# Solved 32x32 blocks brought back by products with the identity, and a filter transform cut in four parts

## What is computed

```
def second_block(x, ...):
    for i in range(2):
        x = x + 0.5 * swiglu(rmsnorm(x))
        # projections of rmsnorm(x)
        o_dn = deltanet_group(q, k, v, z, beta, alpha)   # 4 heads, both directions
        o_hy = hyena_group(...)                           # 2 long convolutions
        x = x + concat([o_dn, o_hy]) @ w_out
        x = x + 0.5 * swiglu(rmsnorm(x))
```

```
a_mat = where(strict, (k * beta) @ k.T * decay, 0) + eye(c)
u, w  = triangular_solve(a_mat, [v * beta, k * beta * exp(g)])
```

## Time and profile before

| | us |
|---|---|
| median of three runs | 3780.5 |
| the profiled execution: its time | 3779.45 |
| the profiled execution: its span in the trace | 3777.7 |
| TensorE busy | 3666.6 |
| VectorE busy | 2021.8 |
| ScalarE busy | 1081.1 |
| GpSimd busy | 70.8 |

### The profile page before, as it was taken

How to read it: one execution, slowest core, us unless ns; L and a number is a source line. 1 busy time by engine, 2 the same in 40 slices (tenths; PEclk the granted TensorE clock), 3 DMA queues, 4 the chain that set the end, 5 groups by cost and what they waited for, 6 DMA issues and landing times.

```text
span 3777.7 us, 43120 instructions
## 1 busy us (share of the span) xinstructions
PE 3666.6 (97%) x17650; PEld 2965.0 (78%) x17650; DVE 2021.8 (54%) x2565; ACT 1081.1 (29%) x1212; POOL 70.8 (2%) x80
## 2 busy tenths in 40 slices
PE   9999999999999999999998899999999998999998
PEld 8878888867788887888876678888888875768887
DVE  6564434454654445434775865434443767675432
ACT  3342222252422222222343132222222243322221
POOL 0000000000000000000010000000000102000000
PEclk9999999999999999999999999999999999999999
DMA  4212222111222222223312122222222413122221
GB/s 150 102 67 93 96 92 101 70 44 45 90 96 100 89 101 89 100 95 113 122 32 95 79 96 93 100 92 98 100 89 100 144 56 101 68 78 93 97 95 73
DMA packets 67764, 342.99 MB, mean 91 GB/s; under 512 B 23748, under 2 KB 23748, under 8 KB 32048
## 3 DMA queue, kind: packets, MB, share of 16 engines
q1 hardware_dynamic: 59696, 302.98, 22.7%
q0 software_dynamic: 5760, 37.86, 2.7%
q10 hardware_dynamic: 2176, 0.26, 0.0%
HBM read 324.30 MB, written 16.78 MB: 90 GB/s over the span
## 4 chain that ended last, share of the span: by engine, by line
PE 87%; DVE 10%; ACT 2%; issue 1%; DMA 1%; ACTq 0%; SPq 0%; DVEq 0%
PE ACC L1020 26%; PE ACC L1022 26%; PE ACC L1021 26%; DVE BX L3031 1%; DVE BT L3029 1%; DVE PT L3224 1%; PE ACC L1446 1%; DVE PT L3222 1%; PE MIX L1760 0%; DVE WL L2385 0%; PE MIX L1497 0%; PE ACC L1692 0%; PE MIX L1333 0%; PE MIX L1517 0%; PE MIX L1205 0%
## 5 line engine op out<-in xcount | busy, mean ns | idle before, releaser
L1020 PE MATMUL ACC<-HH,WH 128*128 128x512 f32 (+1 forms) x3322 | 1303.3, 392 | 19.4 <-issue 6.5
L1022 PE MATMUL ACC<-HH,WL 128*128 128x512 f32 (+1 forms) x3322 | 1288.0, 388 | 0.0
L1021 PE MATMUL ACC<-HL,WH 128*128 128x512 f32 (+1 forms) x3322 | 1287.9, 388 | 0.0
L2385 DVE TENSOR_TENSOR WL<-RAW,WH 128x2048 fp32r<-128x2048 f32 (+3 forms) x291 | 645.6, 2218 | 461.1 <-ACT WH L1854 460.6
L1020 PEld LDWEIGHTS ACC<-HH,WH 128*128 128x128 f32 x3322 | 624.8, 188 | 165.7 <-issue 18.2
L1021 PEld LDWEIGHTS ACC<-HL,WH 128*128 128x128 f32 x3322 | 625.2, 188 | 130.2 <-issue 5.0
L1022 PEld LDWEIGHTS ACC<-HH,WL 128*128 128x128 f32 x3322 | 625.1, 188 | 128.7
L1854 ACT ACTIVATE WH<-RAW 128x2048 fp32r<-128x2048 f32 (+3 forms) x291 | 536.1, 1843 | 578.8 <-PE ACC L1022 578.6
L2505 DVE TENSOR_TENSOR SG<-ACC,RS 128x512 f32<-128x512 f32 x132 | 91.3, 691 | 627.1 <-PE ACC L1022 626.8
L1020 PE MATMUL ACC<-HIDH,WH 128*128 128x512 f32 x1056 | 410.8, 389 | 0.0
L1021 PE MATMUL ACC<-HIDL,WH 128*128 128x512 f32 x1056 | 410.8, 389 | 0.0
(11 more groups left out here) (521 smaller groups left out, 2834.2 us busy)
## 6 DMA issues: line engine op xcount, KB each, us to landing
RAW<-wall SPq DMA_DIRECT2D x260, 1024.0 KB, 4.7
RAW<-wall SPq DMA_DIRECT2D x24, 768.0 KB, 4.1
KR<-spectra POOLq DMA_DIRECT2D x4, 2048.0 KB, 9.2
x_kept<-X POOLq DMA_DIRECT2D x2, 2048.0 KB, 6.6
FWK<-mats POOLq DMA_DIRECT2D x4, 1024.0 KB, 5.4
spectra<-SQ POOLq DMA_DIRECT2D x8, 512.0 KB, 3.0
spectra<-T POOLq DMA_DIRECT2D x8, 512.0 KB, 3.5
X<-x_kept POOLq DMA_DIRECT2D x2, 2048.0 KB, 14.5
```

What stands on the lines that cost most here:

```text
L1020: pe.matmul(out_ap, wh, hh, start=first, stop=False)
L1021: pe.matmul(out_ap, wh, hl, start=False, stop=False)
L1022: return pe.matmul(out_ap, wl, hh, start=False, stop=last)
L2385: v.tensor_tensor(WL[n % 2][:, 0:cols], RAW[n % 2][:, 0:cols], WH[n % 2][:, 0:cols], ALU.subtract).then_inc(w_lo, 1)
```

## The change

The trip through DRAM is gone: `blocks_out`, `blocks_back` and their semaphores, the issues of SyncE and ScalarE. In its place:

- `turn_solved` on TensorE: for each of 32 columns x, both directions d and four blocks b, a product of a 32x32 piece of `BX` with 16 columns of the identity, written to banks 2 (direction 0) and 3 (direction 1) of ACC. That is 256 products, each 32 contraction rows, 32 output rows, 16 columns. It waits for `blocks_solved` and for ScalarE to have emptied ACC.
- `solved_forward` on VectorE: four copies of 32 partitions x 512 elements from bank 2 into the diagonal blocks of `XI[:, 0]`; four of the same size on ScalarE from bank 3 into `XI[:, 1]`. `left` now waits for both (`xi_fwd`, `xi_bwd`) and no longer for the transposes; `right` waits for the transposes (`dn_xt`). For direction 1 `XI` is now filled and `XIT` is the transpose, so GpSimd clears `XI[:, 1]`, after the first two parts of the last transform (`kf_half`) and after the issue of two more stores.
- the last `filter_spectrum(1, 1)` is cut in four parts of two products each: two ahead of `turn_solved`, one behind it, one between `left` and `right` of level 0. Both `keep_clock` are gone. On ScalarE `keep_spectrum(1, 1)` goes behind the two `copy_left`.
- `YS` of the first half of the heads gets a place of its own, since the old one lies over the tables that the last parts of the transform still read.

```
-                    sp.wait_ge(blocks_solved, L + 1)
-                    sp.dma_start(blocks_out, BX[:]).then_inc(solved_sent, 16)
-                    sp.wait_ge(solved_sent, 16 * (L + 1))
-                    sp.wait_ge(dn_zero, 3 * L + 3)
-                    blocks_back(sp, 0, 0)
-                    blocks_back(sp, 1, 0)
-                    blocks_back(sp, 1, 1)
...
-                        if n == 4:
-                            pool.wait_ge(kf_sp, 4 * l + 2)
-                            pool.memset(XIT[:, 1], 0.0).then_inc(dn_zero, 1)
+                        if n == 6:
+                            pool.wait_ge(kf_half, l + 1)
+                            pool.memset(XI[:, 1], 0.0).then_inc(dn_zero, 1)
...
+        def diagonal(d, b):
+            rows = slice(64 * d + 32 * (b // 2), 64 * d + 32 * (b // 2) + 32)
+            return rows, slice(64 * d + 16 * b, 64 * d + 16 * b + 16), slice(32 * b, 32 * b + 32)
+        def solved_in(d, b):
+            return ACC[32 * b:32 * b + 32, 2 + d, :].rearrange("p (x m) -> p m x", m=16)
...
+                def turn_solved():
+                    pe.wait_ge(blocks_solved, L + 1)
+                    pe.wait_ge(kf_ev, 8 * L + 6)
+                    for x in range(32):
+                        for d in range(2):
+                            for b in range(4):
+                                held, wanted, to = diagonal(d, b)
+                                col = BX[held, :, x] if d == 0 else BX[held, x, :]
+                                mm = pe.matmul(ACC[to, 2 + d, 16 * x:16 * x + 16], col, ident[held, wanted], start=True, stop=True)
+                    mm.then_inc(solved_turned, 1)
...
-                for o in range(2):
-                    for fc in range(2):
-                        filter_spectrum(o, fc)
-                pe.wait_ge(kf_ev, 8 * L + 6)
-                keep_clock(ACC[:, 0, :], 12)
+                filter_spectrum(0, 0)
+                filter_spectrum(0, 1)
+                filter_spectrum(1, 0)
+                pe.wait_ge(kf_ev, 8 * L + 4)
+                spectrum_part(1, 1, 0, 0)
+                spectrum_part(1, 1, 0, 1).then_inc(kf_half, 1)
+                turn_solved()
+                spectrum_part(1, 1, 1, 0)
                 left(0, 0, 0)
                 left(0, 1, 0)
-                pe.wait_ge(kf_ev, 8 * L + 8)
-                keep_clock(MIX[:, 0, :], 10)
+                spectrum_part(1, 1, 1, 1).then_inc(kf_sp, 1)
                 right(0, 0, 0)
...
                 grown_keys(0, 0)
                 act.wait_ge(dn_zero, 3 * L + 3)
-                act.wait_ge(solved_sent, 16 * (L + 1))
-                blocks_back(act, 0, 1)
-                keep_spectrum(1, 1)
+                act.wait_ge(solved_turned, L + 1)
+                for b in range(4):
+                    rows = slice(32 * b, 32 * b + 32)
+                    k = act.activation(XI[rows, 1, :, rows], solved_in(1, b), ACT.Copy)
+                k.then_inc(xi_bwd, 1)
                 copy_left(0, 0, 0)
                 copy_left(0, 1, 0)
+                keep_spectrum(1, 1)
                 grown_keys(0, 1)
...
+                def solved_forward():
+                    v.wait_ge(solved_turned, L + 1)
+                    for b in range(4):
+                        rows = slice(32 * b, 32 * b + 32)
+                        k = v.tensor_copy(XI[rows, 0, :, rows], solved_in(0, b))
+                    k.then_inc(xi_fwd, 1)
+                    v.wait_ge(xi_fwd, L + 1)
...
                 def turn_blocks(p):
-                    v.wait_ge(solved_landed[p], 128 * (L + 1))
-                    v.wait_ge(kf_sp, 4 * L + 4)
+                    v.wait_ge(xi_bwd, L + 1)
```

More of the change, by code:

```diff
@@ L678, in build @@
         blocks_solved = sem("blocks_solved")
-        solved_sent = sem("solved_sent")
-        solved_landed = [sem(f"solved_landed{i}") for i in range(2)]
+        solved_turned = sem("solved_turned")
+        xi_fwd = sem("xi_fwd")
+        xi_bwd = sem("xi_bwd")
+        kf_half = sem("kf_half")
         dn_xt = sem("dn_xt")
@@ L858, in build @@
         KG = put("KG", [P, 2, 2, TC, P])
-        YS = put("YS", [P, 2, 2, TC, P])
+        YS = [place("YS0", [P, 2, 2, TC, P], at=raw_at + 4 * 4096), put("YS1", [P, 2, 2, TC, P])]
         assert put.at[0] <= mem_at
         blocks_in = nc.dram_tensor("blocks_in", (P, 32, 32), F32).ap()
-        blocks_out = nc.dram_tensor("blocks_out", (P, 32, 32), F32).ap()
         put = arena(hy_low)
@@ L1401, in left @@
                     if lev == 0:
-                        pe.wait_ge(dn_xt, 4 * L + h + 1)
+                        pe.wait_ge(xi_fwd, L + 1)
+                        pe.wait_ge(xi_bwd, L + 1)
                         pe.wait_ge(dn_at, 4 * L + h + 1)
@@ L1419, in right @@
                     if lev == 0:
+                        pe.wait_ge(dn_xt, 4 * L + h + 1)
                         for c in range(TC):
@@ L1422, in right @@
                                 for near, far in joined(d, lev):
-                                    mm = pe.matmul(ACC[far, 2 * a + d, columns(c, near)], XIT[far, d, TC * h + c, far], YS[far, a, d, c, near],
+                                    mm = pe.matmul(ACC[far, 2 * a + d, columns(c, near)], XIT[far, d, TC * h + c, far], YS[p][far, a, d, c, near],
                                                    start=True, stop=True)
@@ L1434, in right_turned @@
                             for near, far in joined(d, lev):
-                                mm = pe.matmul(ACC[near, 2 * a + d, columns(c, far)], YS[far, a, d, c, near], XIT[far, d, TC * h + c, far],
+                                mm = pe.matmul(ACC[near, 2 * a + d, columns(c, far)], YS[p][far, a, d, c, near], XIT[far, d, TC * h + c, far],
                                                start=True, stop=True)
@@ L1518, in filters_made, with spectrum_part @@
                     mm.then_inc(kf_f, 1)
+                def spectrum_part(o, fc, cs, p):
+                    bank = (ACC, MIX)[fc]
+                    for kc in range(2):
+                        q = 2 * p + kc
+                        src = FS0[:, cs, q, :] if o == 0 else FS1[:, q, :] if cs == 0 else (FS1A, FS1B)[q // 2][:, q % 2, :]
+                        mm = pe.matmul(bank[:, 2 * cs + p, :], FWK[:, cs, p, kc, fc * P:fc * P + P], src,
+                                       start=(kc == 0), stop=(kc == 1))
+                    return mm
                 def filter_spectrum(o, fc):
-                    bank = (ACC, MIX)[fc]
                     if o == 0:
@@ L1528, in filter_spectrum @@
                         for p in range(2):
[L1529 to L1533, removed]
-                    mm.then_inc(kf_sp, 1)
+                            mm = spectrum_part(o, fc, cs, p)
+                    mm.then_inc(kf_sp, 1)
+                def turn_solved():
[8 more added lines that the diff above has]
+                    mm.then_inc(solved_turned, 1)
                 sums_of_g(0)
@@ L1579, in pe_delta @@
                 pe.wait_ge(dn_qe, 8 * L + 8)
+                pe.wait_ge(kf_ev, 8 * L + 8)
                 values(0, 0)
@@ L2161, in copy_left @@
                     act.wait_ge(dn_y, 8 * L + 4 * p + 2 * lev + a + 1)
-                    act.activation(YS[:, a].rearrange("p d c n -> p d (c n)"), ACC[:, 2 * a:2 * a + 2, :], ACT.Copy).then_inc(dn_yc, 1)
+                    act.activation(YS[p][:, a].rearrange("p d c n -> p d (c n)"), ACC[:, 2 * a:2 * a + 2, :], ACT.Copy).then_inc(dn_yc, 1)
                 def copy_keys(p, a):
@@ L3041, in turn_blocks @@
                         v.transpose(XIT[:, 0, m].rearrange("p c n -> p (c n)"), XI[:, 0, m].rearrange("p c n -> p (c n)"))
-                        v.transpose(XI[:, 1, m].rearrange("p c n -> p (c n)"), XIT[:, 1, m].rearrange("p c n -> p (c n)")).then_inc(dn_xt, 1)
+                        v.transpose(XIT[:, 1, m].rearrange("p c n -> p (c n)"), XI[:, 1, m].rearrange("p c n -> p (c n)")).then_inc(dn_xt, 1)
                 def corner(tile, a, h, d, rows, cols):
@@ L3107, in dve_delta @@
                 solve_blocks()
+                solved_forward()
                 turn_blocks(0)
```

## The result

The changed kernel is slower: 3785.67 us median of 20 runs against 3777.93 us of 20 runs of the kernel before. The ratio is 1.0019, 95% interval 1.0013 to 1.0026, so 7.7 us with an interval of about 5 to 10. The forecast was 3778.3 us beside a median of 3780.5 us, so 2.2 us faster; over 20 runs that median is 2.6 us lower, and only the differences can be compared: 2.2 us faster was forecast, 7.7 us slower came. The time lies inside the stated range. At 0.19% it stands on the border of the forecast's classes "within 0.2%" (0.61) and "slower" (0.17), with an interval that is clear of no change.

A forecast was written before the change was run, and what follows sets the result against it. TensorE, busy 97% of the span, was taken as the bound. 3779.45 - 3.0 (way from "solved" to right) + 0.8 (clock charge) = 3777.25 us, or 3778.3 us beside the runs' median; range 3769.5 to 3790 us.

The forecast's parts named there:

- within 0.2%: Outcome class: a time within about 0.2% (7.6 us), which a measurement can't tell from no change; chance 0.61.
- slower: Outcome class: slower than the kernel before by more than about 0.2% (7.6 us); chance 0.17.
- Step 2: turn_solved's burst of 512 pairs: 5.6 us at full clock (11 ns a pair), 7.2 us with most at half.
- a burst over 9 us: Sign of being wrong: turn_solved's 512 pairs take over 9 us, where 5 to 8 us would show the forecast right.
- a slow fetch of the 1024 added instructions: Rival, joined with both transform parts at half clock: no gain, 3780 to 3784 us; joint chance 0.20.
- Steps 1, 3 and 4: Half the transform ends just ahead of "solved"; PSUM copies take 2.65 us on VectorE; TensorE's list, not data, releases right.
- step 5: Clock falls to half 1.2 us into the burst, returns about the third part's end; layers gain 3.0 us to right.
- Step 6: Behind right the 8.84 us to keys_solved stay; 0.4 us a layer charged for the full clock's uncertain return.
- The products don't overlap: Rival: turn_solved pairs on the same array rows run singly, 31 ns each, 15.6 us burst; 3793 to 3799 us; chance 0.16.
- The clock holds: Rival: small tiles without a pause keep TensorE at full clock; 3769 to 3773 us; chance 0.24.

The follow-up runs named there:

- loop: Changed kernel with turn_solved as a loop of 8 turns over the same 4 columns plus one more column, 528 pairs: 3777.18 us, ratio 0.9998.
- half: Changed kernel without the products of 16 of the 32 columns of turn_solved, 256 pairs a layer in place of 512: 3770.21 us, ratio 0.9985.
- rows_change: Changed kernel with the same products reordered so that neighbours never use the same 32 rows of the array: 3783.92 us, ratio 1.0017.
- idle_burst: vector_turn with the 256 products put back on TensorE ahead of the dummies and left, read by nobody: 3793.25 us, ratio 1.0041.
- idle_loop: idle_burst with the products as a loop of 8 turns over four columns and one column more, 528 pairs: 3780.33 us, ratio 1.0010.
- vector_turn: Changed kernel with blocks turned by two VectorE transposes instead of TensorE products, TensorE and ScalarE orders changed too: 3765.99 us, ratio 0.9964.
- cut_alone: Kernel before, DRAM trip kept, with only the last transform cut in parts, second keep_clock gone, keep_spectrum and YS moved: 3776.22 us, ratio 0.9994.

## Why the prediction was wrong, by its steps

- **Step 2, the burst, is the one that failed.** I took the pace of bursts of 32 and 64 pairs (11 to 15 ns) for 512 pairs and said 7.2 us. The pace was right, 11.7 ns, even at half clock, where I had 15. The three pauses were missing: 7.4 and 6.1 us. Layer 0 took 13.2 us, 6.0 more than forecast, layer 1 4.7 more, 10.7 us in all. The prediction has a gain of 3.0 us for the way to `right` and the traces a loss of 7.9: 10.7 of the 10.9 us between them are this step. Of the prediction's signs of being wrong it is the one that came, "a burst over 9 us". Where nearly no code is new (loop), 528 pairs took 7.6 us, close to my 7.2 for 512: the array was priced well, and what I put at nothing was the arrival of the code. That the pauses are the fetch of code is shown by one run that keeps the number of products and takes the code away (loop), one that halves both (half), one that changes only the order of the products (rows_change), and by the pair idle_burst and idle_loop, where nothing waits for the results. The trace's packets say the same: each of the 20 pauses inside the bursts of the changed kernel, half, rows_change and idle_burst ends 1.2 to 1.6 us after a packet of the fetch queue has landed.
- I had named "a slow fetch of the 1024 added instructions" beside a rival worth 3780 to 3784 us, without a price of its own. The rows for one were there: the page's 98 packets with 1.61 MB make 16 KB a packet, and 1024 instructions are four of these; in this kernel 256 instructions had never been executed in less than several us, so no row showed how fast such packets can follow. The right bound would have been open above, and the rival a separate one. In its cause this rival was the right one; against the median it started from it gave at most 3.5 us lost, and 7.7 came.
- Steps 1, 3 and 4 held, and step 5 in the main. Half of the transform ended at "solved". VectorE's copies took 2.79 us (2.65), ScalarE's 2.38 (2.4). The clock fell 2.9 us into the burst of layer 0, where I had 1.2, and in a pause of TensorE that I hadn't foreseen; in loop, without pauses, it fell 4.4 us in. It came back at the end of the third part in layer 0, and 1.2 us later, at the end of `left`, in layer 1. From the end of the burst to `right`: 6.1 us in layer 0 and 6.7 in layer 1 (6.25). ScalarE's slack ahead of the level-1 `copy_left` was 1.01 us (1 us).
- Step 6: from `right` to `keys_solved` 8.84 us, as before. `keys_solved` took 4.77 us for 5.82 in layer 0 and 5.27 for 5.79 in layer 1; the return of the full clock came earlier, a gain of 1.6 us in all where I had charged 0.8. This error has the other sign and hides a part of step 2's.
- The 3202.05 us that I gave for `right` in layer 1 is 3202.02 in the timeline; the 14.6 us stand.
- *The products don't overlap*, the slower rival, gave the right direction and too high a time, by a mechanism that rows_change excludes. That the measured time lies inside the range is luck: the range was wide on that side for this rival. *The clock holds* is excluded by the window at 0.50 and, since TensorE stood still for most of that one, better by loop, where the clock fell under tiles without a pause.
- The gain of the rest was real: with the burst gone and the blocks turned by VectorE, the same idea is worth 0.36% (vector_turn, which also changes the order of the last parts on TensorE and ScalarE). The cut of the transform alone showed no gain clear of the noise (cut_alone).

## What to carry to other kernels

Count the instructions that a change adds to one stretch of an engine's list, not only their durations: on TensorE here a packet of 256 instructions (128 pairs of load and matmul, 64 float32 products) came every 3.5 to 4.8 us inside the bursts, 27 to 38 ns a pair, where the pairs took 12 ns. The straight-line bursts of small products paid this beyond their first 151 to 231 pairs. The 128x512 products at 0.43 us a pair showed no such pause, and a loop over the same code nearly none of its own, though code behind it came late once in each layer (idle_loop). Turning the blocks on VectorE took two instructions a layer in place of 1024. A pace read from a burst of 64 pairs is no pace for 512.

## What the runs showed of the hardware that was not expected

- The first run of a burst is 151 to 231 pairs long (159 and 231 in the changed kernel), every later full one 128. In layer 0 a packet's transfer takes 0.9 to 1.4 us, while the runs start 3.45 and 3.73 us apart, so most of the cycle isn't the transfer itself: the next transfer begins only 1.0 to 1.2 us after a run has begun, and the next run 1.2 to 1.6 us after that transfer has landed. Why the next packet isn't asked for earlier stays open. The Trainium skill, "Runtime: NRT & Kernel Launch", section "Instruction fetch mechanics", says that TensorE's instruction memory holds 2048 instructions, refilled in blocks of 256, and that the fetch is hidden because instructions are issued more slowly. The blocks of 256 agree with the trace. The rest doesn't here: TensorE had been on pairs of 0.43 us for over 20 us before and still stood still after 318 instructions.
- The Trainium skill's floor of 25 ns from start to start ("TensorE: Matmul & The Clock Gate", section "Wait — 56ns, not 53.3ns?") isn't one for these 32x32 tiles: 128 pairs in 1.48 us, 11.6 ns, at half clock with 16 columns, and 11.7 ns at full clock with 32.
- ScalarE's copy of 32x512 took 0.60 us out of PSUM and 1.08 us out of SBUF, while VectorE's four took 2.79 and 2.42 us. The order of the walk isn't the cause, nor is it that source and target lie in different partitions, since the fourth copy of vector_turn goes from partitions 96 to 127 into the same and took 1.06 us too. The step of the source (64 bytes out of PSUM, 128 out of SBUF) and the memory itself weren't separated, so the cause stays open.
- VectorE's 32x32 transposes of 64x1024 took 1.24 us with a contiguous source and 1.94 us with a stepped one (1.93 to 2.03 us over the runs).
